# Last block's attention: jobs of two heads in turn, products three slots behind the scores, more buffers

## The reference, cut to what matters

```
s = concat_g(q[g,h,b] @ k[g,h].T / 8 + bias[g,h]);  p = exp(s - max(s))
o[b,h] = concat_g(p) @ concat_g(v[g,h]) / sum(p)
```

## Time and profile before

| | us |
|---|---|
| median of 3 runs | 3617.72 |
| the profiled execution's own time | 3616.14 |
| its span, first to last instruction | 3614.6 |
| busy in the span: PE | 3538.0 |
| DVE | 1941.9 |
| ACT | 1468.7 |

### The profile page before, as it was taken

One profiled execution on the slowest core, in us unless ns is written; L12 is line 12 of the kernel. 1 busy time (PEld: TensorE's weight loads), 2 busy tenths in 40 slices (PEclk: granted clock), 3 DMA queues, 4 the chain that ended last, 5 costly groups with the idle time before them and its releaser, 6 DMA issues.

```text
span 3614.6 us, 48067 instructions
## 1 busy us (share of the span) xinstructions
PE 3538.0 (98%) x17468; PEld 2820.4 (78%) x17468; DVE 1941.9 (54%) x3237; ACT 1468.7 (41%) x2190; POOL 174.2 (5%) x181
## 2 busy tenths in 40 slices
PE   8999999999999999999999999999999999999998
PEld 6888886657888888888866577888887887878886
DVE  4443475767544344434657765544379775545433
ACT  4442245654443234322355544443233333534431
POOL 0000000000100000000000001000000001020001
PEclk9999999999999999999999999999999999999999
DMA  3223432104333222334221043323322221313231
GB/s 136 97 95 103 140 111 68 51 27 169 137 99 99 99 100 97 99 101 139 91 94 56 27 158 134 101 99 99 121 93 83 68 78 66 125 64 110 93 103 66
DMA packets 98397, 351.96 MB, mean 97 GB/s; under 512 B 11663, under 2 KB 11919, under 8 KB 97736
## 3 DMA queue, kind: packets, MB, share of 16 engines
q1 hardware_dynamic: 84384, 304.35, 25.4%
q0 software_dynamic: 7040, 23.66, 1.8%
q10 hardware_dynamic: 6824, 21.95, 1.8%
HBM read 333.08 MB, written 24.70 MB: 99 GB/s over the span
## 4 chain that ended last, share of the span: by engine, by line
PE 87%; DVE 8%; ACT 3%; issue 2%; DMA 0%; POOLq 0%; POOL 0%; ACTq 0%; DVEq 0%
PE bank L276 24%; PE bank L278 23%; PE bank L277 23%; PE bank L557 5%; PE bank L1615 1%; PE bank L1642 1%; DVE unit_lo L272 1%; PE bank L989 1%; PE bank L1018 1%; PE bank L998 1%; ACT unit_hi L267 1%; DVE val L1791 1%; PE bank L1631 1%; PE bank L1090 1%; PE bank L1035 1%
## 5 line engine op out<-in xcount | busy, mean ns | idle before, releaser
L272 DVE TENSOR_TENSOR unit_lo<-unit_raw,unit_hi 128x1024 fp32r<-128x1024 f32 x540 | 663.8, 1232 | 719.8 <-ACT unit_hi L267 709.5
L276 PE MATMUL bank<-h_hi,unit_hi 128*128 128x512 f32 x2416 | 951.8, 394 | 11.7 <-DVE unit_lo L272 7.1
L278 PE MATMUL bank<-h_hi,unit_lo 128*128 128x512 f32 x2416 | 943.0, 390 | 0.0
L277 PE MATMUL bank<-h_lo,unit_hi 128*128 128x512 f32 x2416 | 942.7, 390 | 0.0
L267 ACT ACTIVATE unit_hi<-unit_raw 128x1024 fp32r<-128x1024 f32 x540 | 567.2, 1052 | 391.5 <-PE bank L278 379.0
L276 PEld LDWEIGHTS bank<-h_hi,unit_hi 128*128 128x128 f32 x2416 | 455.3, 188 | 109.1 <-DVE unit_lo L272 8.5
L278 PEld LDWEIGHTS bank<-h_hi,unit_lo 128*128 128x128 f32 x2416 | 455.0, 188 | 96.3
L277 PEld LDWEIGHTS bank<-h_lo,unit_hi 128*128 128x128 f32 x2416 | 455.4, 188 | 94.9 <-issue 1.7
L276 PE MATMUL bank<-act_hi,unit_hi 128*128 128x512 f32 x880 | 346.7, 394 | 0.0
L278 PE MATMUL bank<-act_hi,unit_lo 128*128 128x512 f32 x880 | 345.0, 392 | 0.0
L277 PE MATMUL bank<-act_lo,unit_hi 128*128 128x512 f32 x880 | 341.5, 388 | 0.0
(11 more groups left out here) (304 smaller groups left out, 4595.9 us busy)
## 6 DMA issues: line engine op xcount, KB each, us to landing
unit_raw<-in_units SPq DMA_DIRECT2D x572, 512.0 KB, 3.3
gates_kept<-gate_z POOLq DMA_DIRECT2D x32, 256.0 KB, 2.3
sig_ab<-gates_kept ACTq DMA_DIRECT2D x16, 512.0 KB, 3.8
bias_rows<-bias_once POOLq DMA_DIRECT2D x2, 3840.0 KB, 18.8
x_kept<-x ACTq DMA_DIRECT2D x2, 2048.0 KB, 11.1
x<-x_kept ACTq DMA_DIRECT2D x2, 2048.0 KB, 8.6
bias_t<-bias_rows POOLq DMA_DIRECT2D x16, 256.0 KB, 3.2
x<-in_x SPq DMA_DIRECT2D x4, 512.0 KB, 7.7
```

What stands on the lines that cost most here:

```text
L272: nc.vector.tensor_tensor(w_lo[u % SLOTS][:], raw[u % SLOTS][:], w_hi[u % SLOTS][:].bitcast(F32), ALU.subtract).then_inc(unit_lo, 1)
L276: nc.tensor.matmul(out_ap, w_h, r_h, start=first, stop=False)
L277: nc.tensor.matmul(out_ap, w_h, r_l, start=False, stop=False)
L278: return nc.tensor.matmul(out_ap, w_l, r_h, start=False, stop=last)
```

## The change

Jobs n and n+1 (n even) are now the two heads of a pair for the same block. Their six score matmuls are issued in two bursts of three, in the order (job n, group 0), (n+1, 0), (n, 1) and (n+1, 1), (n, 2), (n+1, 2), on banks 2, 3 and 4 each time. An even slot t has burst 0 after the first of its four k-steps and burst 1 after the fourth, and burst 1 waits until VectorE has read the three of burst 0. The turns tr(t-2) come after the third k-step, the value products pv(t-3) after the first, each in a place of its own. ScalarE does the copies of turn t-2 and then exp(t-1). VectorE has the even slots' six reductions in two halves with one tap after each, and four taps in the others. There are four `neg_s2` and two `prob2`; some of them lie on x, which ScalarE sends to memory at the start of the stage and fetches at the start of the next. The gate results go through `qk` tiles, and the tail has 11 slots.

```diff
-    neg_s2, prob2, prob_t2 = (blk.tensor(n, 1280) for n in ("neg_s2", "prob2", "prob_t2"))
+    neg_s2, prob2, prob_t2 = (blk.tensor(n, 1280) for n in ("neg_s2_0", "prob2", "prob_t2"))
+    over_x = Place(nc, x_at)
+    neg_s2 = [neg_s2, nc.alloc_sbuf_tensor_at("neg_s2_1", [P, 1280], F32, offset=sq_at)] + [over_x.tensor(f"neg_s2_{i}", 1280) for i in (2, 3)]
+    prob2 = [prob2, over_x.tensor("prob2_1", 1280)]
+    assert over_x.at <= h_hi_at
...
-    TAIL_SLOTS = 10
+    TAIL_SLOTS = 11
...
 
-        return n // 8, n // 4, n % 4
+        return n // 8, n // 8 * 2 + n % 2, n % 8 // 2
...
 
-        def sc(n):
-            p, h, b = job2(n)
-            if n == 0:
+        def sc(n, burst):
+
+            if n == 0 and burst == 0:
                 pe.wait_ge(s["v_out"], 3 * TB)
                 pe.wait_ge(s["glu"], KD)
-            else:
-                pe.wait_ge(s["job_red"], n)
-            pe.wait_ge(s["qk_out"], 6 * (p + 1))
-            for g, (_, w) in enumerate(spans(b)[0]):
+            pe.wait_ge(s["qk_out"], 6 * (n // 8 + 1))
+            if n + burst > 0:
+                pe.wait_ge(s["job_parts"], 3 * n + 3 * burst)
+            for e in range(3 * burst, 3 * burst + 3):
+                g, (p, h, b) = e // 2, job2(n + e % 2)
+                w = spans(b)[0][g][1]
                 half, t, q0 = qk_tile(p, h, 2 * g)
                 _, _, k0 = qk_tile(p, h, 2 * g + 1)
                 first_key = (b + 1) * P - w
-                mm = nc.tensor.matmul(bank[2 + g][:, 0:w], t[half, q0 + b * P:q0 + (b + 1) * P],
+                mm = nc.tensor.matmul(bank[2 + e % 3][:, 0:w], t[half, q0 + b * P:q0 + (b + 1) * P],
                                       t[half, k0 + first_key:k0 + first_key + w], start=True, stop=True)
             mm.then_inc(s["job_sc"], 1)
 
         def tr(n):
-            b = n % 4
+            _, _, b = job2(n)
             pe.wait_ge(s["job_exp"], n + 1)
             if n >= 1:
...
+                    mm = nc.tensor.transpose(bank[5 + g][:, kb * P:(kb + 1) * P], prob2[n % 2][:, at + kb * P:at + (kb + 1) * P], ident)
             mm.then_inc(s["job_tr"], 1)
...
-        def slot(p, t):
-
-            if 0 <= t - 2 < 8:
-                pv(8 * p + t - 2)
-            if t < 8:
-                sc(8 * p + t)
-            if 0 <= t - 1 < 8:
-                tr(8 * p + t - 1)
+        def slot(p, t, lag):
+
+            if lag == 0 and 0 <= t - 3 < 8:
+                pv(8 * p + t - 3)
+            if lag in (0, 3) and t < 8 and t % 2 == 0:
+                sc(8 * p + t, lag // 3)
+            if lag == 2 and 0 <= t - 2 < 8:
+                tr(8 * p + t - 2)
 
         for p in range(PAIRS):
...
                                k == 0, k == KD - 1)
-                    if k == 3 and p > 0:
-                        slot(p - 1, 2 * i)
-                mm.then_inc(unit_used, 1)
-                if p > 0:
-                    slot(p - 1, 2 * i + 1)
+                    if k == KD - 1:
+                        mm.then_inc(unit_used, 1)
+                    if p > 0:
+                        slot(p - 1, 2 * i + k // 4, k % 4)
         for e in range(GATES2):
             u = TAIL_FIRST + e
...
 
     def blk1_act(act, f, r):
         fence(act, f)
         act.dma_start(b2[:], A["block2_columns"]).then_inc(s["mixer_in"], 16)
+        act.dma_start(x_kept, x[:]).then_inc(s["x_sent"], 16)
...
         def slot(p, t):
...
-            if not 1 <= t <= 8:
-                return
-            n = 8 * p + t - 1
-            b = n % 4
-            (c0, c1, c2), width = spans(b)
-            act.wait_ge(s["job_red"], n + 1)
-            if n >= 1:
-                act.wait_ge(s["job_tr"], n)
-            nc.scalar.activation(prob2[:, 0:width], neg_s2[:, 0:width], ACT.Exp, scale=-1.0, bias=neg_m2[:, n:n + 1],
-                                 accum_out=den2[:, n:n + 1]).then_inc(s["job_exp"], 1)
-            act.wait_ge(s["job_tr"], n + 1)
-            if n >= 1:
-                act.wait_ge(s["job_pv"], n)
-            for g, (at, w) in enumerate((c0, c1, c2)):
-                a = nc.scalar.activation(prob_t2[:, at:at + w], bank[5 + g][:, 0:w], ACT.Copy)
-            a.then_inc(s["pt_out"], 1)
+            if 0 <= t - 2 < 8:
+                n = 8 * p + t - 2
+                (c0, c1, c2), _ = spans(job2(n)[2])
+                act.wait_ge(s["job_tr"], n + 1)
+                if n >= 1:
+                    act.wait_ge(s["job_pv"], n)
+                for g, (at, w) in enumerate((c0, c1, c2)):
+                    a = nc.scalar.activation(prob_t2[:, at:at + w], bank[5 + g][:, 0:w], ACT.Copy)
+                a.then_inc(s["pt_out"], 1)
+            if 0 <= t - 1 < 8:
+                n = 8 * p + t - 1
+                _, width = spans(job2(n)[2])
+                act.wait_ge(s["job_red"], n + 1)
+                if n >= 2:
+                    act.wait_ge(s["job_tr"], n - 1)
+                nc.scalar.activation(prob2[n % 2][:, 0:width], neg_s2[n % 4][:, 0:width], ACT.Exp, scale=-1.0, bias=neg_m2[:, n:n + 1],
+                                     accum_out=den2[:, n:n + 1]).then_inc(s["job_exp"], 1)
 
         for p in range(PAIRS):
             for i in range(6):
...
-        act.wait_ge(s["glu"], KD)
...
-            nc.scalar.activation(sq[e % 2][:], bank[e % 2][:], ACT.Copy).then_inc(s["gate_z"], 1)
+            if e == 0:
+                act.wait_ge(s["job_pv"], 8 * (PAIRS - 1))
+            nc.scalar.activation(tile(qk[PAIRS % 2], e % 2), bank[e % 2][:], ACT.Copy).then_inc(s["gate_z"], 1)
...
-        def slot(p, t):
-            if 0 <= t - 2 < 8:
-                n = 8 * p + t - 2
+        def attended(p, t):
+            if 0 <= t - 3 < 8:
+                n = 8 * p + t - 3
                 _, h, b = job2(n)
                 dve.wait_ge(s["job_pv"], n + 1)
                 nc.vector.reciprocal(rden2[:, n:n + 1], den2[:, n:n + 1]).then_inc(s["dve_step"], 1)
                 dve.wait_ge(s["dve_step"], n + 1)
                 nc.vector.tensor_scalar(o2[:, b * 512 + h * HD:b * 512 + (h + 1) * HD], o_bank, rden2[:, n:n + 1], None,
                                         ALU.mult).then_inc(s["o_out"], 1)
-            if t < 8:
-                n = 8 * p + t
-                _, h, b = job2(n)
-                dve.wait_ge(s["job_sc"], n + 1)
-                dve.wait_ge(bias_in[h % 2], 16 * 3 * (h // 2 + 1))
-                if n >= 1:
-                    dve.wait_ge(s["job_exp"], n)
-                for g, (c0, w) in enumerate(spans(b)[0]):
-                    off = (256, 768, 1280)[g]
-                    ins = nc.vector.tensor_tensor_reduce(out=neg_s2[:, c0:c0 + w], in0=bank[2 + g][:, 0:w],
-                                                         in1=bias_t[h % 2][:, off - w:off], scale=-1.0, scalar=3e38,
-                                                         op0=ALU.add, op1=ALU.min, accum_out=neg_m3[:, g:g + 1])
-                ins.then_inc(s["job_parts"], 1)
-                dve.wait_ge(s["job_parts"], n + 1)
-                nc.vector.tensor_reduce(neg_m2[:, n:n + 1], neg_m3[:, 0:3], AX.X, ALU.min).then_inc(s["job_red"], 1)
-                dve.wait_ge(s["job_red"], n + 1)
+
+        def biased(n, burst):
+
+            dve.wait_ge(s["job_sc"], n + burst + 1)
+            for e in ((0, 2, 1), (4, 3, 5))[burst]:
+                g, a, (_, h, b) = e // 2, n + e % 2, job2(n + e % 2)
+                c0, w = spans(b)[0][g]
+                if g == 0:
+                    dve.wait_ge(bias_in[h % 2], 16 * 3 * (h // 2 + 1))
+                    if a >= 4:
+                        dve.wait_ge(s["job_exp"], a - 3)
+                off = (256, 768, 1280)[g]
+                nc.vector.tensor_tensor_reduce(out=neg_s2[a % 4][:, c0:c0 + w], in0=bank[2 + e % 3][:, 0:w],
+                                               in1=bias_t[h % 2][:, off - w:off], scale=-1.0, scalar=3e38,
+                                               op0=ALU.add, op1=ALU.min,
+                                               accum_out=neg_m3[:, 4 * (e % 2) + g:4 * (e % 2) + g + 1]).then_inc(s["job_parts"], 1)
+                if e == 4:
+                    dve.wait_ge(s["job_parts"], 3 * n + 4)
+                    nc.vector.tensor_reduce(neg_m2[:, n:n + 1], neg_m3[:, 0:3], AX.X, ALU.min).then_inc(s["job_red"], 1)
+            if burst == 1:
+                dve.wait_ge(s["job_parts"], 3 * n + 6)
+                nc.vector.tensor_reduce(neg_m2[:, n + 1:n + 2], neg_m3[:, 4:7], AX.X, ALU.min).then_inc(s["job_red"], 1)
+                dve.wait_ge(s["job_red"], n + 2)
+
+        def slot(p, t):
+            attended(p, t)
+            if t < 8 and t % 2 == 0:
+                biased(8 * p + t, 0)
+                convolve(1, KD)
+                biased(8 * p + t, 1)
+                convolve(1, KD)
+            else:
+                convolve(4, KD)
 
         for p in range(PAIRS):
             for i in range(6):
                 u = 28 + 6 * p + i
                 split_lo(dve, r, u + AHEAD)
+                if u == 28:
```

(18 more changed lines are left out.)

## The result

The changed kernel takes 3628.59 us (median of 8 runs, 3627.26 to 3632.35) against 3617.76 of the kernel before on the same chip; the ratio is 1.0032, with a 95% interval of 1.0023 to 1.0041. It is slower by 10.8 us, clear of the 0.2% that can be told. The profiled execution took 3627.55 us for a span of 3625.9.

What follows compares the result with a forecast made beforehand. TensorE, busy 98% of the span, was taken as the bound. Terms -14.4 + 3.6 + 14.2 + 0.9 + 2.6 + 0.5 + 1.4 + 0.2 = +9.0 us on 3617.7 gave 3626.7, range 3612 to 3634.

Steps and rivals of the forecast that it cites:

- the likeliest case: The prediction's main forecast for the whole kernel: +9.0 us, 3626.7, own range 3622 to 3631, chance 0.60.
- Part 1: TensorE's score bursts: two heads' matmuls on different 64-row halves overlap, saving 3.6 us a pair, 14.4 in all.
- Part 2: More boundaries between TensorE's unit matmuls and attention work: adds 0.9 us a pair, 3.6 in all.
- Part 3: Loops: odd value products wait for ScalarE's copies behind the qk copy, adding 14.2 us; pv(6) adds 0.9.
- Part 4: First stall, before burst 1 of job 0: grows from 2.6 to 5.2 us, adding 2.6, plus 0.5 low clock.
- Part 5: VectorE late at pair boundaries and slot 2, second and third loop: adds 1.4 us; last qk copy 0.2.
- Part 6: Remaining changes, such as keeping x in memory, extra buffers, qk tiles and bias loads: no cost.
- Rival B: Odd value products in the loops don't wait: the 14.2 us goes, leaving -5.2, 3612.5; chance 0.15.
- C: Rival: two 64-row score matmuls don't overlap, +14.4 us, 3641; chance 0.04.
- D: Rival: score time halves in full, 8.6 us more saved than forecast, 3618; chance 0.05.
- F: Rival: VectorE stays late, each of 12 even slots in the loops waits 0.6 more, +7, 3634; chance 0.10.

Runs made afterwards that it cites:

- x kept: Kernel before with only x sent to memory at the start of the stage and fetched at the start of the next; 3617.95 us, ratio 1.0001.
- bursts on one half: Changed kernel with burst 0 made of job n's three scores and burst 1 of job n+1's, each on the same 64 rows; 3643.59 us.
- two taps: Changed kernel with two convolution taps instead of three in each half unit of p = 0; 3622.86 us, ratio to before 1.0013.
- copies first: Changed kernel with ScalarE's three copies of an odd job's turn moved ahead of the copy to qk in the loops; 3614.80 us.
- both edits: Changed kernel with odd jobs' copies ahead of the copy to qk and two taps per half unit of p = 0; 3607.62 us.
- products later: Changed kernel with value products after the second k-step of a slot instead of the first, ScalarE's order unchanged; 3619.67 us.
- the best version: Changed kernel with both edits, an early small exp to load ScalarE's table, and three taps instead of four in slots 10 and 11; 3605.57 us.

## Why the prediction was right

Forecast were +9.0 us and 3626.7; measured +10.8 and 3628.6, inside the range and inside the own range of the likeliest case. The mechanism was right: the waits of the odd products outweigh what the scores save. The closeness of the number is partly luck: the sections of the change grew by 12.3 us in the profile, of which the low clock in the loops (3.0) and the table load (1.4) had no term, and stretches outside of them happened to be 0.9 shorter. Step by step:

- **Part 1, scores side by side.** 14.4 forecast. The bursts of a loop take 3.7 us less than the scores before, 15.0 in four; taken away, they cost 15.0. Shown. The full halving that the Trainium skill's "Up to 2×" (TensorEngine Tiling (Array Packing), Overview) would allow, by estimate 23 us, isn't reached here: a burst of three leaves one without a partner, and its three matmuls of 512 columns take 1.91 us, the price of two.
- **Part 2, boundaries.** 3.6 forecast with part 1's 14.4, together -2.7 a pair. The tail, where nothing waits before or after, measures it clean: -2.84.
- **Part 3, the odd products.** 4.7 us a loop forecast, 0.67 to 1.42 each. From the unit matmul before it to each of the four products of the second loop are 0.90, 1.21, 1.43 and 1.65 us, of which 0.23 is a unit matmul's step: 0.67, 0.98, 1.20, 1.42; and each restart costs 0.10 more (160 ns to the second matmul instead of 55). That is 4.7 a loop and 14.1 in all. Taking the wait away gave 13.8 us; that this equals the 14.1 is chance, since 0.9 a loop was left or came back elsewhere and about 3 us of the 13.8 are low clock that went too. pv(6): 0.3 forecast, 0.33 measured with its restart.
- **Part 4, the first stall.** 5.2 forecast, 5.15 to 5.3 measured, +2.7 over before. The clock's part was mis-sized. I took 0.5 for it, as more low clock after the longer pause; that part is 0.3 in these two profiles, but with one profile each it isn't known better than to 1.7, by what the profile with x kept shows. (Of the "three such rows" at 0.50 before the change two are; the two beside them show 0.65 and 0.64. Together they cost 1.7 us, not 1.5.) What I had no term for are the two other stretches at 0.50 in the loops, each about 3 us long, about 1.5 us each: the third loop is 1.5 longer than the second with the same waits in it. They make the missing 3 us, or the most of it.
- **Part 5, VectorE at the boundaries.** 0.7 a loop forecast; the gaps in the second loop are 0.47 and 0.66 us less 0.32 for a normal one, 0.5 together, and in the third 0.35 and 0.65, 0.4. Slot 2 of the first loop I had inside of this term; there the wait is 1.8 us, 1.4 of them the table load's way through `split_hi`. The prediction doesn't name the table load. Before the change it was hidden in the stall; after it the first exp sits in another slot, with `split_hi` behind it.
- **Part 6.** The copies of x cost nothing: 3617.95 against 3617.66.

With the terms as measured: -15.0 + 3.6 (parts 1 and 2: four times -2.85) + 14.1 + 1.0 (part 3) + 2.7 + 0.3 (part 4) + 0.9 + 0.2 (part 5) + 1.4 (the table load) + 3.0 (the clock in the loops) = +12.2, against +12.3 in the table of sections.

Rival B (no wait) is excluded by the waits' rows; its number, 3612.5, is near what the kernel becomes when the wait is really taken away, 3614.8. C is excluded by the bursts on one half, D by the widths, F by 0.5 us where it wanted 7. What remains open is what makes the clock fall in the loops. Ahead of the fall at 2827 TensorE had waited 1.2 us at a product and was in a run of 16 small ones; ahead of that at 2978, 1.4 us and 20. The second loop has the same waits and no fall. All three kernels with the twelve full waits (the changed one, two taps, bursts on one half) have two such stretches in the loops of their profiles; the four with fewer or shorter ones (copies first, both edits, products later, the best version) have none, apart from that after the first stall where the stall is left. That ties them to the waits but doesn't show which, and no run was made for it alone. It isn't the waits alone either: in earlier stages, whose code is the same in all, four of the ten profiles show a fall near 1820 or 1831 us and the others none.

## What to carry to other kernels

Where an engine works through a fixed order, a result is ready only when everything ahead of it in that order is done: follow each hand-over through the middle engine's queue, with what that engine itself waits for there, before you shift the two ends by half a step. On a path with no idle time a 0.7 to 1.4 us wait at every second hand-over ate all that a real saving of array time had brought, and one reordered line gave it back. Look also for what a stall was hiding (here a table load): it shows once the stall is gone.

## What the runs showed of the hardware

- Two fp32 matmuls on different 64-row halves start 6 to 7 ns apart in the trace and run in the time of one; three of 512 columns in the order of halves 1, 0, 1 take 1.91 us instead of 2.77.
- A value product after a wait of TensorE has 160 ns to its second matmul instead of 55.
- Waits of 1.2 to 1.4 us between dense matmuls can be followed by some 3 us at half clock, 1.5 us lost, in one loop and not in the next of the same shape. Behind the same stall of 2.45 us the low clock lasted about 3 us in one profile and 7 in another.
- A function table load of 1.28 us on ScalarE, far from TensorE, held TensorE up by 1.4 us by way of the next `split_hi` and VectorE's `unit_lo`; an earlier exp took that away.
